# Two reorderings in a fused two-block kernel: first masks ahead of a token shift in the recurrent mixer, value transposes behind the first query group and late value products later in attention

## The chip, the cores and the metric
One Trainium2 chip, one core. The metric is the device time of one execution in microseconds (us); lower is better. Its engines run programs of their own, in order, and meet through semaphores: TensorE (PE in the profile; its weight loads are PEld), VectorE (DVE), ScalarE (ACT), GpSimd (POOL) and SyncE (SP), which only issues the weight transfers here.

## The reference, cut to what matters
Two transformer blocks in f32 over 256 tokens (272 with 16 meta tokens in the first block) of width 2048. Block one is a mixer, half short convolution and half a recurrence (RWKV-7: sixteen heads of 64), and a gated feed-forward with a convolution. Block two is a sliding-window attention with 32 query heads, 8 key heads and a sink per head, and a feed-forward of the same kind.

```python
def step(s, inp):                      # the recurrence, per head
    r_t, w_t, k_t, v_t, a_t, b_t = inp
    sa = jnp.einsum('bhvk,bhk->bhv', s, a_t)
    s = s * w_t[:, :, None, :] + sa[..., None] * b_t[:, :, None, :] + v_t[..., None] * k_t[:, :, None, :]
    return s, jnp.einsum('bhvk,bhk->bhv', s, r_t)
...
q, k, v = split_cols(h @ w_in, SWA_SPLITS)
s = einsum(q, kb) * HEAD_DIM ** -0.5 + bias          # masked to the window
p = softmax(concatenate([s, sink]))[..., :-1]
o = einsum(p, vb)
return o @ w_out
```

## The kernel before, in words
Every projection is `x @ W` with f32 weights that stream in as 512 KB chunks (two blocks of 128 rows by 512 columns). A ring of `RING = 4` chunks is filled by SP (`raw`). For each chunk ACT writes a rounded copy (`high`, line 525, tile `wh`) and DVE the rest (`low`, line 899, tile `wl`); TensorE multiplies in three passes, high by high, low by high, high by low. `high(n)` waits for the landing of chunk n and until TensorE has used chunk n-3 (`chunk_used`); `low(n)` waits for `high(n)` (`high_ready`); TensorE waits for `low(n)` (`low_ready`). Each engine's calls of `highs` and `lows` stand at fixed places among its other work, so a wait in one call holds back everything behind it on that engine.

**Mixer.** Projection groups 0 to 6 give the columns of the recurrence; group 6 holds the values v. `z_read(6)` (line 1007) takes them out of PSUM and `z_shift(6)` blends neighbouring tokens (a difference, line 1014, and four updates, line 1018, the last of which raises `z_ready`). The recurrence runs in five chunks of up to 64 tokens (c = 0 to 4). For each, TensorE makes the Gram products (line 1874) in banks 4 to 7, DVE masks them (`gak`, `grk`: `k_masked`; then `am`, `ga`, `grb`: `b_masked`; lines 1247 to 1253), TensorE turns four tiles by products with an identity (`heads`, line 1797: k into bank 6, am into 7, v into 4, b into 5), and a chain of levels l (products P, joins J) inverts the masked matrix. Between these steps TensorE is given pieces of the remaining projections, halves of chunks (`fill`, lines 1786 to 1788). `inverse_lengths(c, half)` (lines 1056 and 1058: a maximum and a reciprocal) serves a later chunk; `refill(s)` on DVE does a piece of the convolution and the `low` conversions that are due in that slot.

**Attention.** The projection `in2` has six groups of eight chunks: group 0 keys, group 1 values, groups 2 to 5 queries. The first two are interleaved over in2 chunks 0 to 15; group 2 has chunks 16 to 23. Its first half runs, then eight transposes of the values (line 1973) go to banks 4 and 5, ACT copies them out (`vt`, line 842), the second half follows, and TensorE waits for `vt_ready` before the loop. DVE's program here is: read group 0, `lows` of chunks 17 to 20, read group 1, `lows` of 21 to 26, and only then `evacuate_in2(2)` (line 1500), which raises `q_first` for the first scores. Neither version changes that DVE order. The loop has 18 turns over 16 pairs of heads. In turn i TensorE has `values(i-2)` (line 2037), `scores(i)` (line 2017), a piece of projection (`fill_attention`, lines 1997 to 2002), `turn(i-1)`, the transposes of the normalised weights (line 2028), and a second piece. Turns 0 to 12 have two halves of a chunk in each piece, turns 13 to 15 one in each, turn 16 two and none. ACT does per turn `out_high(i-2)` (line 868), the due `high`s, `softmax_pair(i)` (line 855) and `turn_out(i-1)` (line 863). DVE does `out_low(i-2)` (line 1544), its part of `scores(i)` (lines 1524 and 1526), the due `low`s and `normalise(i)`. `turn(i)` waits for `pn_ready` of pair i and for `o_low` of the pair before it, since both use bank 7.

Of the kernel before, what the change touches and what calls it, by code (L numbers as in the profile page):

```python
# [24 lines left out]
ACT = mybir.ActivationFunctionType  # L25

P = 128
# [116 lines left out]
def program(nc, d):  # L144
    with ExitStack() as ctx:
# [249 lines left out]
        def grams(b):  # L395

            return ps[:, b:b + 2, :].rearrange("p b (f x t) -> p (b f) x t", f=4, x=2)
# [116 lines left out]
        def _(act):  # L514
# [12 lines left out]
            def highs(first, count, slot=0):  # L527
                if isinstance(first, int):
                    count = clamp(first, count)
                for c in range(count):  # L530
                    high(first + c, (slot + c) % RING)
# [305 lines left out]

            bias_src = bass.AP(scratch.tensor, 0, [[1, P], [384, N_HEADS], [1, SEQ]])
            act.dma_start(bias[:], bias_src).then_inc(bias_landed, 16)
            highs(FIRST["in2"] + 19, 4, 3)  # L840
            act.wait_ge(v_turned, 1)
            act.activation(vt[:], ps[:, 4:6, :], ACT.Copy).then_inc(vt_ready, 1)
            highs(FIRST["in2"] + 23, 5, 3)

            def softmax_pair(i):

# [46 lines left out]
        def _(dve):  # L893
# [116 lines left out]
            def z_shift(g):  # L1010
                dve.wait_ge(group_read, g + 1)
                if g:
                    dve.wait_ge(z_ready, g)
                dve.tensor_tensor(zd[:], z[:, 4 * g:4 * g + 4, 0:L], z[:, 4 * g:4 * g + 4, 1:L + 1],
                                  ALU.subtract).then_inc(dve_step, 1)
                dve.wait_ge(dve_step, steps.add())
                for k in range(4 * g, 4 * g + 4):
                    last = dve.scalar_tensor_tensor(z[:, k, 1:L + 1], zd[:, k % 4], vcol("mu", k), z[:, k, 1:L + 1],
                                                    ALU.mult, ALU.add)
                last.then_inc(z_ready, 1)  # L1020
# [100 lines left out]
            factors(0)  # L1121
            lows(55, 5, 3)
            z_read(6)
            z_shift(6)
            dve.wait_ge(bias_stored, 16)

            def conv_read(s):
# [115 lines left out]
            for c in range(N_RC):  # L1243
                s = SLOT[c, "gram"]
                conv_read(s)
                dve.wait_ge(gram_done, 2 * c + 1)
                dve.tensor_tensor(gak[:], grams(6)[:, :, 0], over(gmask[:, 0], RT), ALU.mult)
                dve.tensor_tensor(grk[:], grams(6)[:, :, 1], over(gmask[:, 1], RT), ALU.mult).then_inc(k_masked, 1)
                dve.wait_ge(gram_done, 2 * c + 2)
                dve.tensor_tensor(am[0][:], grams(4)[:, :, 0], over(lmask[:, 0], RT), ALU.mult).then_inc(am_ready, 1)  # L1250
                dve.tensor_copy(ga[:], grams(4)[:, :, 0]).then_inc(dve_step, 1)
                ga_step = steps.add()
                dve.tensor_tensor(grb[:], grams(4)[:, :, 1], over(gmask[:, 1], RT), ALU.mult).then_inc(b_masked, 1)
                dve.wait_ge(am_ready, level(c, 0))
                dve.tensor_tensor(tt[:], am[0][:], over(identc[:], RT), ALU.add).then_inc(tt_ready, 1)
                dve.wait_ge(dve_step, ga_step)
                level_matrix(c, 1)
                refill(s)

                s = SLOT[c, "turn"]  # L1260
                conv_read(s)
                dve.wait_ge(am_turned, c + 1)
                dve.tensor_tensor(tn[:], bank(7), over(identc[:], RT), ALU.add).then_inc(tn_ready, 1)
                if c:
                    bonus_keys(c - 1)
                if c == LAST:
                    bonus_keys(c)
                refill(s)

                for l in range(1, LEVELS[c]):  # L1270
                    s = SLOT[c, f"P{l}"]
                    conv_read(s)
                    if l + 1 < LEVELS[c]:
                        level_matrix(c, l + 1)
                    if l == 3 and c < LAST:
                        factors(c + 1)
                    if c < 2 and l in (1, 4):
                        inverse_lengths(2 * c + 1 + l // 4, 0)
                    if c < 2 and l in (2, 5):
                        unit_keys(2 * c + 1 + l // 5)  # L1280
                    if c and l == 4:
                        inverse_spread(c - 1, 1)
                    if c and l == 5:
                        bonuses(c - 1, 7)
                    refill(s)

                    s = SLOT[c, f"J{l}"]
                    conv_read(s)
                    if l < LEVELS[c] - 1:
                        dve.wait_ge(dn_done, not_last(c, l))  # L1290
                        dve.wait_ge(tn_ready, turned_level(c, l - 1))
                        dve.tensor_tensor(tn[:], tn[:], bank(5), ALU.add).then_inc(tn_ready, 1)
                    dve.wait_ge(dt_done, inner(c, l))
                    dve.wait_ge(tt_ready, level(c, l - 1))
                    dve.tensor_tensor(tt[:], tt[:], bank(6), ALU.add).then_inc(tt_ready, 1)
                    if c < 2 and l in (1, 4):
                        inverse_lengths(2 * c + 1 + l // 4, 1)
                    if c and l == 3:
                        inverse_spread(c - 1, 0)
                    if 0 < c < LAST and l == 4:  # L1300
                        unit_y(c - 1)
                    refill(s)

                s = SLOT[c, "update"]
                conv_read(s)
                if c == LAST:
                    bonuses(c - 1, 7)
                    bonuses(c, 5)
                    inverse_spread(c - 1, 1)
                    unit_y(c - 1)  # L1310
                refill(s)

                s = SLOT[c, "output"]
                conv_read(s)
                if c < LAST:
                    dve.wait_ge(s_done, c + 1)
                    ends = pend[:, c].unsqueeze(2).broadcast_to([P, RT, C])
                    if c:
                        dve.wait_ge(st_ready, c)
                        dve.tensor_tensor(st[:], st[:], bank(5), ALU.add).then_inc(dve_step, 1)  # L1320
                        dve.wait_ge(dve_step, steps.add())
                    dve.tensor_tensor(st[:], st[:] if c else bank(5), ends, ALU.mult).then_inc(st_ready, 1)
                else:
                    gated_bonus(TG, TA, LAST - 1)
                    gated(TG, TA, LAST - 1)
                refill(s)
# [258 lines left out]
        def _(pe):  # L1585
# [272 lines left out]
            for c in range(N_RC):  # L1858
# [24 lines left out]
                pe.wait_ge(am_ready, level(c, 0))  # L1883
                heads(7, [(lambda f: am[0][:, f], lambda f: identc[:])], am_turned)
                pe.wait_ge(b_masked, c + 1)
                pe.wait_ge(z_ready, 7)
                heads(4, [(lambda f: z[:, 20 + f, 1 + t0:1 + t0 + n], lambda f: identc[:])], vb_turned, rows=n)
                if c < LAST:
                    heads(5, [(lambda f: bk[:, f, 0], lambda f: identc[:])], b_turned)
                finish(c, "turn")  # L1890

# [74 lines left out]
                chunks_of("in2", n0, n0 % RING, 0, x_of(SEQ), SEQ, range(c0, c1))  # L1966

            pe.wait_ge(group_read, G0["in2"] + 1)
            in2_piece(2, 0, 4)
            pe.wait_ge(group_read, G0["in2"] + 2)  # L1970
            for kb in range(2):
                for g2 in range(4):
                    last = pe.transpose(ps[:, 4 + kb, P * g2:P * (g2 + 1)], vf[:, g2, QB * kb:QB * (kb + 1)], ident[:])
            last.then_inc(v_turned, 1)
            in2_piece(2, 4, 8)
            pe.wait_ge(vt_ready, 1)

            def fill_attention(part):

# [40 lines left out]
            def turn(i):  # L2020
                pe.wait_ge(pn_ready, i + 1)
                if i:
                    pe.wait_ge(pt_ready, i)
                    pe.wait_ge(o_low, i)
                for e in range(2):
                    for t, col in enumerate((0, QB + 1, 2 * QB + 1)):
                        x = 3 * e + t
                        last = pe.transpose(ps[:, 6 + x // 4, QB * (x % 4):QB * (x % 4 + 1)], pr[:, i % 2, e, col:col + QB], ident[:])
                last.then_inc(p_turned, 1)
# [12 lines left out]
            for i in range(N_PAIRS + 2):  # L2042
                if i == N_PAIRS + 1:
                    fill_attention(WEAVE_FILL[i][0])
                if i >= 2:
                    values(i - 2)
                if i < N_PAIRS:
                    scores(i)
                if i <= N_PAIRS:
                    fill_attention(WEAVE_FILL[i][0])  # L2050
                if 1 <= i <= N_PAIRS:
                    turn(i - 1)
                fill_attention(WEAVE_FILL[i][1])
# [119 lines left out]
```

## Time and profile before

| what | value |
|---|---|
| median of 3 runs | 2430.51 us (2430.29 to 2430.63) |
| the profiled execution's own time | 2430.03 us |
| its span, first to last instruction | 2428.2 us |
| TensorE busy | 2385.4 us, 98% |
| DVE / ACT / POOL busy | 1522.2 / 1038.2 / 167.3 us |
| mean granted TensorE clock | 0.997 of full |
| bytes moved | 406.04 MB, mean 167 GB/s |

A time in the rows is counted from the start of the span. An engine's idle time matters here only where it ends in idle time of TensorE.

### The profile page before, as it was taken

The page shows a single profiled execution, that of the slowest core. Times are in us where ns is not written, and L with a number is a line of the kernel's source. Part 1 is how long each engine was busy: PE and PEld are TensorE (multiplying, and loading weights), DVE is VectorE, ACT ScalarE, POOL GpSimd, SP SyncE. Part 2 cuts the span into 40 slices and gives each one's busy share as a digit, 9 for nine tenths or more (in the row PEclk, how much of TensorE's full clock was granted, in tenths as well). Part 3 has the DMA queues.
Part 4 walks back from the last instruction along what each step waited for, and adds up shares of the span by engine and source line. Part 5 has one row for each costly group of instructions (what it writes and reads, how often), then busy time and mean ns, then how long its engine had stood idle before and what let it go on. Part 6 is the DMA issues. An engine that isn't in the chain of part 4 may idle for free.

```text
span 2428.2 us, 54209 instructions
## 1 busy us (share of the span) xinstructions
PE 2385.4 (98%) x21898; PEld 2294.9 (95%) x21898; DVE 1522.2 (63%) x1951; ACT 1038.2 (43%) x1292; POOL 167.3 (7%) x197
## 2 busy tenths in 40 slices
PE   7999999999999999999999999999999999999996
PEld 7999999999999999999889999899999999998896
DVE  6577665665866666565444666647767667664444
ACT  5543333344544443444444456555444344344442
POOL 2000000001400000000000310015000000000001
PEclk9999999999999999999999999999999999999998
DMA  7443222345455555555555473354555555555553
GB/s 240 153 163 123 82 89 91 112 142 183 148 191 181 184 182 180 186 183 183 189 186 189 148 252 131 117 179 154 191 185 179 190 184 179 191 186 188 190 185 104
DMA packets 116224, 406.04 MB, mean 167 GB/s; under 512 B 12624, under 2 KB 19760, under 8 KB 115824
## 3 DMA queue, kind: packets, MB, share of 16 engines
q1 hardware_dynamic: 109248, 392.22, 49.4%
q10 hardware_dynamic: 6832, 11.68, 1.4%
q8 instruction: 118, 1.93, 0.3%
q14 instruction: 26, 0.21, 0.0%
HBM read 401.69 MB, written 2.15 MB: 166 GB/s over the span
## 4 chain that ended last, share of the span: by engine, by line
PE 93%; DVE 4%; ACT 1%; issue 1%; ACTq 0%; DVEq 0%
PE ps L1637 17%; PE ps L1638 17%; PE ps L1639 17%; PE ps L1633 11%; PE ps L1635 6%; PE ps L1797 5%; PE ps L1786 2%; PE ps L1609 2%; PE ps L1610 2%; PE ps L1611 2%; PE ps L1788 2%; PE ps L1787 2%; DVE wl L899 1%; PE ps L2000 1%; DVE h L1382 1%; PE ps L2002 1%
## 5 line engine op out<-in xcount | busy, mean ns | idle before, releaser
L899 DVE TENSOR_TENSOR wl<-raw,wh 128x1024 fp32r<-128x1024 f32 x744 | 915.5, 1239 | 761.0 <-ACT wh L525 760.4
L525 ACT ACTIVATE wh<-raw 128x1024 fp32r<-128x1024 f32 x744 | 781.0, 1057 | 1036.0 <-PE ps L1639 558.6
L1637 PE MATMUL ps<-xh,wh 128*128 128x256 f32 (+2 forms) x3456 | 979.6, 283 | 18.9 <-DVE xl L924 18.2
L1638 PE MATMUL ps<-xl,wh 128*128 128x256 f32 (+2 forms) x3456 | 976.6, 283 | 0.0
L1639 PE MATMUL ps<-xh,wl 128*128 128x256 f32 (+2 forms) x3456 | 976.3, 282 | 0.0
L1637 PEld LDWEIGHTS ps<-xh,wh 128*128 128x128 f32 x3456 | 652.9, 189 | 22.5 <-DVE wl L899 16.2
L1638 PEld LDWEIGHTS ps<-xl,wh 128*128 128x128 f32 x3456 | 653.9, 189 | 0.2
L1639 PEld LDWEIGHTS ps<-xh,wl 128*128 128x128 f32 x3456 | 652.5, 189 | 0.0
L1633 PE MATMUL ps<-act,wh 128*128 128x512 f32 x1056 | 369.7, 393 | 0.0
L1635 PE MATMUL ps<-act,wl 128*128 128x256 f32 x1056 | 294.6, 279 | 0.0
L1633 PEld LDWEIGHTS ps<-act,wh 128*128 128x128 f32 x1056 | 197.8, 187 | 47.3
L1635 PEld LDWEIGHTS ps<-act,wl 128*128 128x128 f32 x1056 | 197.9, 187 | 0.0
L1786 PE MATMUL ps<-xh,wh 128*128 128x260 f32 x384 | 114.6, 298 | 1.1 <-DVE cg L1142 0.9
L1787 PE MATMUL ps<-xl,wh 128*128 128x260 f32 x384 | 108.3, 282 | 0.0
L1788 PE MATMUL ps<-xh,wl 128*128 128x260 f32 x384 | 108.2, 282 | 0.0
L445 POOL TENSOR_TENSOR sq_sum<-sq_sum,sq 128x256 f32<-128x256 f32 (+2 forms) x104 | 84.1, 808 | 344.6 <-ACT sq L540 335.5
L1609 PE MATMUL ps<-act,wh 128*128 128x256 f32 x352 | 99.6, 283 | 0.0
L1610 PE MATMUL ps<-act,wh 128*128 128x256 f32 x352 | 99.4, 282 | 0.0
L1611 PE MATMUL ps<-act,wl 128*128 128x256 f32 x352 | 98.7, 280 | 0.0
L463 POOL COPY sq_sum<-sq 128x256 f32<-128x256 f32 (+2 forms) x8 | 4.1, 512 | 1237.4 <-ACT sq L540 1114.7
L1786 PEld LDWEIGHTS ps<-xh,wh 128*128 128x128 f32 x384 | 72.1, 188 | 6.0 <-DVE cg L1142 1.0
L1407 DVE SCALAR_TENSOR_TENSOR cv<-gt,vec,cv 128x256 f32<-128x256 f32 x176 | 73.3, 478 | 0.0
(270 smaller groups left out, 2749.9 us busy)
## 6 DMA issues: line engine op xcount, KB each, us to landing
raw<-in_gate_up SPq DMA_DIRECT2D x176, 512.0 KB, 3.8
raw<-in_down SPq DMA_DIRECT2D x176, 512.0 KB, 4.2
raw<-in_up SPq DMA_DIRECT2D x176, 512.0 KB, 3.8
raw<-in_w_in SPq DMA_DIRECT2D x104, 512.0 KB, 3.7
raw<-in_in SPq DMA_DIRECT2D x48, 512.0 KB, 3.7
raw<-in_w_out SPq DMA_DIRECT2D x32, 512.0 KB, 3.8
raw<-in_out SPq DMA_DIRECT2D x32, 512.0 KB, 3.7
bias<-bias_rows ACTq DMA_DIRECT2D x1, 4096.0 KB, 26.3
```

Source lines behind the costliest of these rows:

```text
L525: act.activation(wh[:, slot], raw[:, slot], ACT.Copy).then_inc(high_ready, 1)
L899: dve.tensor_tensor(wl[:, slot], raw[:, slot], wh[:, slot].bitcast(F32), ALU.subtract).then_inc(low_ready, 1)
L1609: pe.matmul(out, w_high, hi, start=(k == 0), stop=False)
L1610: pe.matmul(out, w_high, lo, start=False, stop=False)
L1633: pe.matmul(ps[:, 4 * parity + m, :], w_high, hi.rearrange("p s n -> p (s n)"), start=(k == 0), stop=False)
L1635: last = pe.matmul(out, w_low, hi[:, 0], start=False, stop=(k == 2 * per - 1))
L1637: pe.matmul(out, w_high, hi, start=(k == 0), stop=False)
L1638: pe.matmul(out, w_high, lo, start=False, stop=False)
L1639: last = pe.matmul(out, w_low, hi, start=False, stop=(k == 2 * per - 1))
L1786: pe.matmul(out, w_high, hi, start=(k == 0), stop=False)
L1787: pe.matmul(out, w_high, lo, start=False, stop=False)
L1788: last = pe.matmul(out, w_low, hi, start=False, stop=(x < 96 and k == KT - 1))
```

## The change
In the mixer, for chunk 0 alone, `z_shift(6)` leaves its place right behind `z_read(6)` and goes behind the mask that raises `b_masked`; TensorE turns b (bank 5) ahead of v (bank 4) in that chunk. In chunks 0 and 1, the second half of `inverse_lengths` goes behind the `refill` of the same slot. In attention all eight chunks of query group 2 run before the value transposes, which now go to banks 6 and 7; ACT makes two more `high`s ahead of the copy of `vt` (19 to 24 instead of 19 to 22) and leaves 25 to 27 behind it; the wait for `vt_ready` moves from ahead of the loop to the first `turn`. In turns 13 to 15 `values(i-2)` goes behind `scores(i)`, and in turn 16 behind the projection piece, straight ahead of `turn(15)`.

```diff
-            highs(FIRST["in2"] + 19, 4, 3)
+            highs(FIRST["in2"] + 19, 6, 3)
             act.wait_ge(v_turned, 1)
-            act.activation(vt[:], ps[:, 4:6, :], ACT.Copy).then_inc(vt_ready, 1)
-            highs(FIRST["in2"] + 23, 5, 3)
+            act.activation(vt[:], ps[:, 6:8, :], ACT.Copy).then_inc(vt_ready, 1)
+            highs(FIRST["in2"] + 25, 3, 1)
...
             z_read(6)
-            z_shift(6)
...
                 dve.wait_ge(gram_done, 2 * c + 1)
+                if c == 0:
+                    dve.wait_ge(group_read, 7)
                 dve.tensor_tensor(gak[:], grams(6)[:, :, 0], over(gmask[:, 0], RT), ALU.mult)
...
                 dve.tensor_tensor(grb[:], grams(4)[:, :, 1], over(gmask[:, 1], RT), ALU.mult).then_inc(b_masked, 1)
+                if c == 0:
+                    z_shift(6)
...
-                    if c < 2 and l in (1, 4):
-                        inverse_lengths(2 * c + 1 + l // 4, 1)
                     if c and l == 3:
                         inverse_spread(c - 1, 0)
                     if 0 < c < LAST and l == 4:
                         unit_y(c - 1)
                     refill(s)
+                    if c < 2 and l in (1, 4):
+                        inverse_lengths(2 * c + 1 + l // 4, 1)
...
                 pe.wait_ge(b_masked, c + 1)
-                pe.wait_ge(z_ready, 7)
+                if c == 0:
+                    heads(5, [(lambda f: bk[:, f, 0], lambda f: identc[:])], b_turned)
+                    pe.wait_ge(z_ready, 7)
                 heads(4, [(lambda f: z[:, 20 + f, 1 + t0:1 + t0 + n], lambda f: identc[:])], vb_turned, rows=n)
-                if c < LAST:
+                if 0 < c < LAST:
                     heads(5, [(lambda f: bk[:, f, 0], lambda f: identc[:])], b_turned)
...
             pe.wait_ge(group_read, G0["in2"] + 1)
-            in2_piece(2, 0, 4)
+            in2_piece(2, 0, 8)
             pe.wait_ge(group_read, G0["in2"] + 2)
             for kb in range(2):
                 for g2 in range(4):
-                    last = pe.transpose(ps[:, 4 + kb, P * g2:P * (g2 + 1)], vf[:, g2, QB * kb:QB * (kb + 1)], ident[:])
+                    last = pe.transpose(ps[:, 6 + kb, P * g2:P * (g2 + 1)], vf[:, g2, QB * kb:QB * (kb + 1)], ident[:])
             last.then_inc(v_turned, 1)
-            in2_piece(2, 4, 8)
-            pe.wait_ge(vt_ready, 1)
...
                     pe.wait_ge(pt_ready, i)
                     pe.wait_ge(o_low, i)
+                else:
+                    pe.wait_ge(vt_ready, 1)
...
                 if i == N_PAIRS + 1:
                     fill_attention(WEAVE_FILL[i][0])
-                if i >= 2:
+                if 2 <= i < 13:
                     values(i - 2)
                 if i < N_PAIRS:
                     scores(i)
+                if 13 <= i < N_PAIRS:
+                    values(i - 2)
                 if i <= N_PAIRS:
                     fill_attention(WEAVE_FILL[i][0])
+                if i >= N_PAIRS:
+                    values(i - 2)
                 if 1 <= i <= N_PAIRS:
                     turn(i - 1)
```

## Rows read from the trace of the kernel before

**Rows 1.** The page: the chain of work that ended last, by engine.
```profile
PE 93%; DVE 4%; ACT 1%; issue 1%; ACTq 0%; DVEq 0%
```

**Rows 2.** Busy time by engine in attention turns 2 to 12 (columns: PE, PEld, DVE, ACT, POOL, clock, DMA).
```profile
1460.00:1550.00 90.00, 90.00 (x802) 82.41 (x802) 62.91 (x182) 54.46 (x133) 2.11 (x11) 1.00 0.40 129
```

**Rows 3.** Timeline, TensorE, mixer chunk 0 (start, duration, operation, count, idle before and releaser).
```profile
207.42 1.15 PE L1797 MATMUL ps<-identc,bk 64*64 64x64 f32 x32 [1.17 <-DVE grk L1248]
...
211.29 0.39 PE L1786 MATMUL ps<-xh,wh 128*128 128x260 f32 x1
```

**Rows 4.** Timeline, DVE, the same stretch.
```profile
203.09 1.29 DVE L1014 TENSOR_TENSOR zd<-z 128x1088 f32<-128x1088 f32 x1
...
206.68 0.68 DVE L1248 TENSOR_TENSOR grk<-ps,gmask 128x512 f32<-128x512 f32 x1
...
209.07 0.68 DVE L1255 TENSOR_TENSOR tt<-am,identc 128x512 f32<-128x512 f32 x1
```

**Rows 5.** Timeline, DVE, mixer chunk 0: the convolution's read behind level 4.
```profile
247.11 1.23 DVE L1142 TENSOR_TENSOR cg<-ps,rstd 128x1040 f32<-128x1040 f32 x1
```

**Rows 6.** Timeline, TensorE, value transposes and first scores of attention.
```profile
1433.83 1.04 PE L1973 MATMUL ps<-ident,vf 128*128 128x128 f32 x8
1434.63 0.36 PE L1637 MATMUL ps<-xh,wh 128*128 128x256 f32 x1
...
1445.97 0.27 PE L1639 MATMUL ps<-xh,wl 128*128 128x256 f32 x1
1446.85 0.93 PE L2017 MATMUL ps<-kf,qf 64*128 64x128 f32 x8 [0.61 <-DVE qf L1500]
```

**Rows 7.** Timeline, ACT: the copy of the turned values and the conversion behind it.
```profile
1434.91 1.03 ACT L842 ACTIVATE vt<-ps 128x1024 f32<-128x1024 f32 x1 [2.58 <-PE ps L1973]
1435.83 1.05 ACT L525 ACTIVATE wh<-raw 128x1024 fp32r<-128x1024 f32 x1
```

**Rows 8.** Timeline, DVE: conversion of in2 chunk 26, then the first query read.
```profile
1444.61 1.23 DVE L899 TENSOR_TENSOR wl<-raw,wh 128x1024 fp32r<-128x1024 f32 x1 [1.63 <-ACT wh L525]
1446.28 0.42 DVE L1500 SCALAR_TENSOR_TENSOR qf<-ps,rstd 128x256 f32<-128x256 f32 x1 [0.45 <-PE ps L1639]
```

**Rows 9.** Timeline, TensorE, attention turns 14 to 16.
```profile
1556.94 0.88 PE L2037 MATMUL ps<-pt,vt 128*64 128x128 f32 x12 [0.47 <-ACT pt L863]
1557.74 0.93 PE L2017 MATMUL ps<-kf,qf 64*128 64x128 f32 x8
...
1560.11 0.81 PE L2028 MATMUL ps<-ident,pr 128*128 128x128 f32 x6
1560.68 0.48 PE L1997 MATMUL ps<-yy,wh 128*128 128x512 f32 x1
...
1568.68 0.88 PE L2037 MATMUL ps<-pt,vt 128*64 128x128 f32 x12 [0.47 <-ACT pt L863]
...
1572.40 0.82 PE L2028 MATMUL ps<-ident,pr 128*128 128x128 f32 x6
```

**Rows 10.** Timeline, DVE, `out_low` in turn 14.
```profile
1558.28 0.42 DVE L1544 TENSOR_TENSOR yy<-ps,yy 128x256 fp32r<-128x256 f32 x1 [0.83 <-ACT yy L868]
```

**Rows 11.** Granted clock after the last matmul; matmul starts at both levels of it.
```profile
2409.00:2412.80 3.80, 0.00 (x1) 0.00 (x0) 3.18 (x4) 0.47 (x1) 1.42 (x2) 1.00 0.00 0
2413.00:2414.00 1.00, 0.00 (x0) 0.00 (x0) 1.00 (x2) 0.00 (x0) 1.00 (x2) 0.50 0.00 0
...
15.38 0.57 PE L1637 MATMUL ps<-xh,wh 128*128 128x272 f32 x1 [15.38 <-DVE xl L924]
...
19.60 0.43 PE L1637 MATMUL ps<-xh,wh 128*128 128x272 f32 x1
19.83 0.43 PE L1638 MATMUL ps<-xl,wh 128*128 128x272 f32 x1
...
20.23 0.29 PE L1637 MATMUL ps<-xh,wh 128*128 128x272 f32 x1
20.35 0.29 PE L1638 MATMUL ps<-xl,wh 128*128 128x272 f32 x1
```

## The prediction, written before the changed kernel had been run

> **What bounds the kernel now.** I read the page first. Its chain of work that ended last runs 93% of the span on TensorE [rows 1]: the time changes only where TensorE idles more or less. The stretch view of attention turns 2 to 12 shows what that is like: TensorE busy 90.00 of 90.00 us, at full clock [rows 2], so nothing moved inside it can gain. Then I looked in TensorE's timeline for idle gaps at the places of the change. There are five. One of 1.17 us stands ahead of the first turned tiles of mixer chunk 0, ended by the mask `grk` [rows 3]. One of 0.61 us stands ahead of the first scores, ended by the first query read [rows 6]. Three of 0.47 us stand ahead of `values` in turns 14, 15 and 16, ended by ACT's `turn_out` (two of the three are shown, and the middle one is like them) [rows 9]. Together that is 3.2 us, 0.13% of the time, and a little more in starts, because a gap counts from the modelled end of a matmul that the next would have overlapped. Measurement tells apart about 0.2%, 4.9 us. So the gains are small whatever happens, and the question is what the moves cost.
>
> **Part 1, masks ahead of the shift (mixer, chunk 0).** On DVE the shift's five instructions run from 203.09, and `grk` ends at 206.68 + 0.68 = 207.36; TensorE starts 0.06 later [rows 3, 4]. The change permutes ten DVE instructions without adding one: five of the shift, five of the masks. From `zd` at 203.09 to `tt` at 209.07 the total stays the same [rows 4], so `grk` ends near 204.4, `grb` near 206.2, the shift's last update near 209.15, and all behind it on DVE keeps its time. TensorE's gap goes: k, am and b are turned from 206.2 to 209.0 (three of four sets, which take (211.29 - 207.42) / 4 = 0.97 us each [rows 3]), then v waits for the shift until about 209.2, a new wait of 0.2 us, and the next piece starts at 209.2 + 1.03 = 210.25 instead of 211.29. Gain 1.0 us. What else could be late: ACT's copies of k, v and b (`kt`, `vb`, `bt`), but a 3 us projection piece lies between them and their users. Without that cover the gain would shrink by ACT's two copies, some 1.2 us. Bounds: 0.6 to 1.1.
>
> **Part 2, reciprocals behind `refill`.** At level 1 no conversion is due in that slot (chunk 0), or none and no convolution step (chunk 1): the order of instructions is unchanged. At level 4 of chunk 0 the order tt, reciprocal, `wl`, `cg` becomes tt, `wl`, reciprocal, `cg`; TensorE waits there for `cg`, which starts at 247.11 [rows 5], and the same work stands ahead of it. In chunk 1 only a 16-column reciprocal moves. Zero, from -0.3 to +0.3.
>
> **Part 3, transposes behind query group 2.** The eight transposes take 1434.63 - 1433.83 = 0.80 us [rows 6]. Moved behind the group, they could cover the wait for the first query read: the scores start at 1446.85 where they could have started at 1445.97 + 0.12 [rows 6], a gain of 0.76 us. But look at what is queued behind ACT's copy. Before, the copy was done at 1435.94 and the conversions 23 to 27 went on [rows 7], so DVE finished its conversion 26 at 1444.61 + 1.23 = 1445.84 and then waited only for TensorE before it read the queries at 1446.28 [rows 8]. After, `high` 25, 26 and 27 stand behind the copy, the copy waits for the transposes, and the transposes stand behind the whole group. DVE still has `low` 25 and `low` 26 ahead of the first query read, and the scores wait for that read. So a chain starts that TensorE cannot cover, as its next instruction is the scores:
>
> - transposes start at 1445.97 + 0.12 - 0.80 = 1445.27 (the group now runs on through the place they left)
> - copy: 1434.91 - 1433.83 = 1.08 later [rows 6, 7], 1446.35
> - `high` 25: 0.92 behind the copy's start [rows 7], 1447.27, ready at 1448.32
> - `low` 25: 1448.36; `low` 26 about 1.13 behind it (its 1.23 busy less the 0.1 by which such neighbours overlap [rows 7, 8]), 1449.5; `high` 26 (from 1448.2 to 1449.25) is in time
> - query read: 1450.6; the scores follow a query read's start by 1446.85 - 1446.28 = 0.57 [rows 6, 8], 1451.15
>
> Against 1446.85 that is 4.3 us late. TensorE idles from the transposes' end, 1445.27 + 1.04 = 1446.3, to 1451.15: 4.85 us, with two ready chunks (24 and, late, 25) lying behind the scores in its order. From there everything in the loop keeps its distances, since turns 2 to 12 hold no slack on TensorE to win it back [rows 2]. SP's queue: the transfers of chunks 29 and 30 wait for `low` 25 and 26 and go out some 6 us later, for conversions due later still; bound 0 to 0.5 us. Bounds of the part: +3.9 (if conversions pack closer) to +5.0. I take 4.3.
>
> **The clock.** After the last matmul of the kernel, at 2409.00, the granted clock stayed at full until past 2412.8 and was half at 2413, some 3.9 us on [rows 11]. The new gap is 4.85 us, longer than that by 1 us. At the kernel's start matmuls ran at half clock (1.2 GHz) from 15.38 to about 20.1, 4.75 us, 0.23 apart, then 0.12 apart [rows 11]. So, if the clock falls, work goes at about 0.53 of its rate for a stretch; 4.75 us of it cost 4.75 x 0.47 = 2.2 us. Bounds 0 and 2.2; as the gap exceeds the 3.9 us by only 1 us, I take a short fall, 1.0 us. The Trainium skill (TensorE: Matmul & The Clock Gate, What's actually happening) says that the throttled clock is the default and only activity releases it; by that the clock may fall or hold here depending on where the gap lies, which no row before decides, and the sum would be 1.0 us less or 1.2 us more than mine.
>
> **Part 4, `values` later (turns 13 to 16).** The three waits come from a closed loop: `values(i-2)`, `out_high`, `out_low`, DVE's scores of pair i, softmax, `turn_out(i-1)`, `values(i-1)`. Its period is (1568.68 - 1556.94) / 2 = 5.87 us [rows 9], while TensorE's own work in a turn is 1560.68 - 1556.94 = 3.74 plus one more piece. A piece of one half is 1560.11 - 1557.74 less the scores' 0.86 (their 0.93 busy less the overlap of 0.07 that values show too), 1.5, and the turn's work 5.24. Every edge of the loop is a data dependence or the order on ACT and DVE, and none is changed. What changes is the start: `values(11)` goes behind scores, 1557.74 - 1556.94 = 0.80 for values and 0.86 for scores, so the loop starts 0.86 later. In turns 14 and 15 TensorE waits as before, now between scores and values. In turn 16, `values(14)` no longer waits, since the two-half piece goes ahead; but `turn(15)` stands right behind it and needs `out_low(14)`, whose end is 1558.28 + 0.42 - 1556.94 = 1.76 us behind the start of `values` [rows 9, 10], of which TensorE covers 0.80 by values themselves. The sum, from the start of turn 13 to `turn(15)`: before, 3 x 5.87 + (1572.40 - 1568.68) = 21.33 [rows 9]; after, 0.86 + 2 x 5.87 + 0.80 + 1.5 + 0.57 + 1.5 + 2.9 + 1.8 = 21.7 (waits of the loop, `values(13)`, a piece, `turn(14)`, a piece, the two halves of turn 16 as 3.72 - 0.80, and `values(14)` to the end of `out_low(14)`). A loss of 0.35, bounds -1.9 (all three waits gone, 3 x 0.63) to +1.0.
>
> **Rivals.** *The clock holds through the gap* (2434.2): for it, that the fall after the last matmul took 3.9 us and the gap has 4.85; against it, the same two numbers. *The clock stays down as long as at the start*: +2.2, 2436.4. *Part 4 works*: the waits vanish, 0.35 becomes -1.9, 2433.0; against it is the closed loop, whose length the rows give. *The other side, faster*: the conversions 25 and 26 do not gate the scores. That would need the copy to begin 4.3 us before I put it, at 1442.0, while the group still runs; from there on the transposes cover the query read and part 3 gives -0.8. With part 1 and 4 as summed it is 2429.1, and with part 4 at its best 2426.8, not even then 0.2% faster. Nothing in the rows speaks for it: only a copy that need not wait for the group's end would do it. *The change does nothing visible* would take the same.
>
> **How the numbers follow.** Against the profiled execution (2430.03, of which the span is 2428.2 and 1.8 lies around it) the sum is -1.0 + 0 + 4.3 + 0.35 + 1.0 = +4.7; the median of the runs is 0.5 above that execution, so 2430.5 + 4.7 = 2435.2. Chances: short fall of the clock 0.40 (2434.6 to 2436.2); clock holds 0.31 (2433.8 to 2434.7); long fall 0.17 (2435.8 to 2437.2); part 4 works 0.06; conversions do not gate 0.04; the rest 0.02. The bound to slower is 2435.4: the long fall lies above it, nearly half of the short one, and a little of the holding case: 0.38. Faster needs under 2425.6: 0.02. Range 2433.4 to 2437.0, which leaves out the last cases and the upper end of the long fall.
>
> **What would show it.** Right: TensorE's first turned tile at 206.2 with a short wait ahead of the turned v; a gap of about 4.8 us ahead of the first scores, released by DVE's query read, with two conversions right ahead of that read on DVE and the copy ahead of them on ACT; two waits for `pt` of about 0.5 us in turns 14 and 15 and one of 0.9 to 1 us ahead of `turn(15)`, released by DVE's `yy`; the granted clock under 1 somewhere near 1450. Wrong: first scores near 1446, or a clock that stays at half for tens of microseconds.

## The result, and the profile after

The changed kernel takes 2435.97 us (median of 11 runs, 2435.12 to 2437.0) against 2430.49 us of the kernel before (11 runs): ratio 1.0021, 95% interval 1.0012 to 1.0030. It is slower by about 0.2%; 2435.2 was forecast, with a range of 2433.4 to 2437.0. Its profiled execution took 2435.20 us, of which the span is 2433.4. In the experiments below, two single executions took 3206.37 us (part 4 alone) and 5030.39 us (part 2 alone) and are left out of their ratios, though not of their medians.

In the changed kernel's lines `values` is line 2042, scores 2020, the value transposes 1978, `turn` 2033, the query read 1503, `out_low` 1547, DVE's scores 1527 and 1529; `heads` is 1800, the mixer's pieces 1789 to 1791. The timeline of TensorE in mixer chunk 0 answers to [rows 3]:

```profile
206.19 1.15 PE L1800 MATMUL ps<-identc,bk 64*64 64x64 f32 x32
207.18 1.10 PE L1800 MATMUL ps<-identc,am 64*64 64x64 f32 x32
208.11 1.10 PE L1800 MATMUL ps<-identc,bk 64*64 64x64 f32 x32
209.34 1.15 PE L1800 MATMUL ps<-identc,z 64*64 64x64 f32 x32
...
210.41 0.39 PE L1789 MATMUL ps<-xh,wh 128*128 128x260 f32 x1
```

The gap of 1.17 us ahead of the first turned tile is gone, b is turned ahead of v, and v waits a little (1.23 us from b to v, where neighbours stand 0.93 to 0.99 apart). The next piece of projection (called the mixer piece below) starts 0.88 us earlier.

TensorE at the value transposes answers to [rows 6]:

```profile
1444.43 1.04 PE L1978 MATMUL ps<-ident,vf 128*128 128x128 f32 x8
1450.25 1.18 PE L2020 MATMUL ps<-kf,qf 64*128 64x128 f32 x8 [4.79 <-DVE qf L1503]
...
1458.48 0.93 PE L2020 MATMUL ps<-kf,qf 64*128 64x128 f32 x8
```

A new idle gap of 4.79 us stands ahead of the first scores, released by DVE's query read. ACT (first fence) and DVE (second) in the same stretch, in place of [rows 7, 8], show why:

```profile
1445.50 1.02 ACT L842 ACTIVATE vt<-ps 128x1024 f32<-128x1024 f32 x1 [8.27 <-PE ps L1978]
1446.42 2.94 ACT L525 ACTIVATE wh<-raw 128x1024 fp32r<-128x1024 f32 x3
```

```profile
1447.51 2.36 DVE L899 TENSOR_TENSOR wl<-raw,wh 128x1024 fp32r<-128x1024 f32 x2 [9.02 <-ACT wh L525]
1449.78 0.41 DVE L1503 SCALAR_TENSOR_TENSOR qf<-ps,rstd 128x256 f32<-128x256 f32 x1
```

ACT waited 8.27 us for the transposes with three conversions behind that wait; DVE waited 9.02 us for the first of them with the query read behind. Both were idle while TensorE ran most of the query group, and then TensorE was idle while they did two conversions that could have been done by then. (`high(n)` needs its ring slot free: the wait is for chunk n-4, one earlier than the section on the kernel before says. So conversion 26 needs chunk 22 and may run while TensorE is at chunk 23, the last of the group; the run with both conversions ahead of the copy, below, shows this: VectorE is at its part of conversion 26 at 1443.06, and the group runs until 1444.54.)

The view of stretches (columns as in [rows 2]: length of the stretch, busy time of PE, PEld, DVE, ACT, POOL, then the granted clock) shows the gap, what follows it, and recovery:

```profile
1445.50:1450.20 4.70, 0.00 (x0) 0.00 (x0) 2.69 (x4) 4.68 (x5) 0.00 (x0) 1.00 0.13 18
1450.90:1454.10 3.20, 3.20 (x17) 2.74 (x14) 2.64 (x10) 1.00 (x5) 0.00 (x0) 0.50 0.73 253
1454.30:1458.00 3.70, 3.70 (x33) 3.70 (x33) 2.27 (x6) 1.73 (x5) 0.19 (x1) 1.00 0.48 142
```

The clock was full through the gap and half (1.2 GHz) behind it: 17 matmuls in 3.20 us, against 33 in 3.70 us right after. From the first to the second scores it is 8.23 us (1450.25 to 1458.48). Before, with the first at 1446.85 [rows 6], it was 6.72:

```profile
1453.57 0.93 PE L2017 MATMUL ps<-kf,qf 64*128 64x128 f32 x8
```

The tail, TensorE in turns 14 to 16, answers to [rows 9]:

```profile
1555.97 0.93 PE L2020 MATMUL ps<-kf,qf 64*128 64x128 f32 x8
1556.83 0.88 PE L2042 MATMUL ps<-pt,vt 128*64 128x128 f32 x12
...
1567.06 0.93 PE L2020 MATMUL ps<-kf,qf 64*128 64x128 f32 x8
1568.35 0.88 PE L2042 MATMUL ps<-pt,vt 128*64 128x128 f32 x12 [0.36 <-ACT pt L863]
...
1575.62 0.88 PE L2042 MATMUL ps<-pt,vt 128*64 128x128 f32 x12
1577.53 0.84 PE L2033 MATMUL ps<-ident,pr 128*128 128x128 f32 x6 [1.03 <-DVE yy L1547]
```

Of three waits for `pt` two are left (one is shown, the other is like it), now between scores and `values`, and a wait of 1.03 us stands ahead of `turn(15)`. Turn 13 began like this before:

```profile
1551.07 0.88 PE L2037 MATMUL ps<-pt,vt 128*64 128x128 f32 x12
```

Added up from the two profiles, as shifts against before: the mixer piece -0.88 (211.29 to 210.41), first scores +3.40 (1446.85 to 1450.25), start of turn 13 +4.90 (1551.07 to 1555.97), `turn(15)` +5.13 (1572.40 to 1577.53), end of span +5.2. The steps between them are the parts: -0.9 mixer, +4.3 the chain ahead of the scores, +1.5 half clock, +0.2 tail. The clock's part differs from one execution to the next, as the section on the scatter shows.

### The profile page after: what moved, and what is told of

Same layout as the page of the kernel before. It is cut to its first block, busy times and chain, and to the rows that moved or that the text cites. A ratio compares the mean times of both kernels' runs of the same rounds, so it can differ in the third digit from the quotient of the medians.

```text
span 2433.4 us, 54204 instructions
## 1 busy us (share of the span) xinstructions
PE 2387.6 (98%) x21898; PEld 2296.5 (94%) x21898; DVE 1521.5 (63%) x1951; ACT 1037.9 (43%) x1292; POOL 167.2 (7%) x197
## 4 chain that ended last, share of the span: by engine, by line
PE 93%; DVE 4%; ACT 1%; issue 1%; POOL 0%; ACTq 0%; POOLq 0%; DVEq 0%
PE ps L1640 17%; PE ps L1641 17%; PE ps L1642 17%; PE ps L1636 11%; PE ps L1638 6%; PE ps L1800 5%; PE ps L1789 2%; PE ps L1612 2%; PE ps L1613 2%; PE ps L1614 2%; PE ps L1790 2%; PE ps L1791 2%; DVE wl L899 1%; PE ps L2003 1%; DVE h L1385 1%
```

## The experiments

The ratios below are to the kernel before, run on the same chip in turn with it. Part 1, part 3, part 4 and the filled gap were run on one chip, the others on a second. On both the kernel before was less steady than above: medians 2431.11 and 2430.63 us, from 2429.7 up to 2434.6. So differences under 1 us are read from the traces, as distances between two points of TensorE's timeline. Such distances repeat to some hundredths where the granted clock is the same in both.

### Part 3 alone

The kernel before with only the lines of the diff from `highs(FIRST["in2"] + 19` to the `vt_ready` wait in `turn`:

```diff
-            in2_piece(2, 0, 4)
+            in2_piece(2, 0, 8)
...
-            in2_piece(2, 4, 8)
-            pe.wait_ge(vt_ready, 1)
```

> The kernel before with part 3 alone: transposes behind query group 2, copy of the turned values behind conversion 24. My theory (two conversions stand behind that copy on ScalarE and ahead of the query read on VectorE): first scores about 5.8 us behind the start of the transposes, a TensorE gap of 4.8 us released by the query read, the start of turn 13 later by 4.2 us less nothing, plus what half clock costs (1.5 us in the changed kernel's profile): 2430.5 + 4.2 + 1.5 to 2.2 = 2436.2 to 2436.9, so more than the whole change. Rival (the loss comes from the moves in the mixer and the late values, or from the sum of all): this part alone gives 2429.7 to 2431.

Measured: 2438.13 us (6 runs, 2435.73 to 2440.88), ratio 1.0031 (1.0018 to 1.0043); the profiled execution took 2436.77. TensorE:

```profile
1446.25 1.03 PE L1973 MATMUL ps<-ident,vf 128*128 128x128 f32 x8
1452.07 1.65 PE L2015 MATMUL ps<-kf,qf 64*128 64x128 f32 x8 [4.79 <-DVE qf L1500]
```

The same 5.82 us from transposes to scores and the same gap, so the rival that the loss comes from the other parts (2429.7 to 2431) is out. Counted from the mixer piece, which starts at 212.32 in this profile, the first scores come 4.19 us later than before (1452.07 - 212.32 against 1446.85 - 211.29), and the second follow after 8.26 us, 1.54 more than before. Together that is 5.7 us, about what the whole change loses in these two steps (4.3 + 1.5). The median is above the expected 2436.2 to 2436.9: three of the six runs lie from 2439.49 to 2440.88, none of them was profiled, and what they hold stays open. By the times alone, part 3 can't be told from the whole change: their intervals overlap.

### Part 1 alone

The kernel before with `z_shift(6)` behind `grb` in chunk 0 and the turned b ahead of v:

```diff
             z_read(6)
-            z_shift(6)
...
+                if c == 0:
+                    z_shift(6)
```

> The kernel before with part 1 alone: chunk 0's masks ahead of the last shift. My theory: the projection piece behind the turned tiles starts 0.9 us earlier and nothing downstream takes it back: 2429.6. Rival (the shift, now behind the masks, makes a later step wait and gives the 0.9 us back): 2430.5.

Measured: 2429.62 us, ratio 0.9995 (0.9986 to 1.0005). The time alone does not settle 0.9 us. The trace does. From the start of `z_read(6)` on DVE to the mixer piece on TensorE it is 8.60 us (202.54 to 211.14), where it was 9.52 before (201.77 to 211.29), a gain of 0.92. And of the kernel before's idle times of TensorE, the one for `grk` is absent and every other is as before (`cg` 0.9, `qf` 0.6, three times `pt`, 1.4 in all), so nothing downstream took the gain back.

### Part 4 alone

```diff
-                if i >= 2:
+                if 2 <= i < 13:
                     values(i - 2)
                 if i < N_PAIRS:
                     scores(i)
+                if 13 <= i < N_PAIRS:
+                    values(i - 2)
...
+                if i >= N_PAIRS:
+                    values(i - 2)
```

> The kernel before with part 4 alone: values behind scores in turns 13 to 15 and behind the piece in turn 16. My theory (a closed loop through ScalarE and VectorE sets the pace; the order on TensorE does not shorten it): from the start of turn 13 to the last turn's transposes 21.5 to 21.7 us against 21.33 before, time 2430.7. Rival (the scores cover the wait): three waits of 0.63 us vanish, 2428.6.

Measured: 2432.39 us, ratio 1.0007 (0.9997 to 1.0016). From the start of turn 13 at 1552.57 to `turn(15)` at 1574.16 it is 21.59 us, 21.33 before: a loss of 0.26 us. TensorE at the end of it:

```profile
1572.26 0.88 PE L2037 MATMUL ps<-pt,vt 128*64 128x128 f32 x12
1574.16 0.85 PE L2028 MATMUL ps<-ident,pr 128*128 128x128 f32 x6 [1.03 <-DVE yy L1544]
```

The medians lie further apart than that, 1.3 us on that chip, and the median is 1.7 us above the expected 2430.7. The profiled execution (2431.84 us) holds a stretch at half clock of its own in the mixer, told of in the last section, so the time is no measure of this part; the distance is. Whether such stretches make up the whole of the difference no run shows.

### The gap filled with dummy matmuls

The changed kernel, with matmuls whose result nobody reads in the gap:

```diff
             last.then_inc(v_turned, 1)
+            for _ in range(19):
+                pe.matmul(ps[:, 4, 0:P], ones[:], ones[:], start=True, stop=True)
```

> The changed kernel with 19 dummy matmuls (a result that nobody reads, in a bank that the scores overwrite) behind the value transposes, some 4.4 us of work inside the 4.8 us gap. If half clock behind the gap costs 1.5 us or more, as the profile of the changed kernel has it: first scores at the same distance from the transposes (5.8 us), granted clock at full throughout, time 2434.0 and the scatter between runs gone. If the clock costs nothing and the scatter has another source: 2435.97, as the changed kernel.

Measured: 2433.95 us, ratio 1.0013 (1.0004 to 1.0022); ten of the eleven runs lie from 2433.25 to 2434.67, and one, not profiled, at 2438.47. TensorE, and the stretch behind the scores:

```profile
1445.27 4.41 PE L1981 MATMUL ps<-ones 128*128 128x128 f32 x38
1450.22 0.93 PE L2022 MATMUL ps<-kf,qf 64*128 64x128 f32 x8 [0.54 <-DVE qf L1503]
```

```profile
1450.90:1458.00 7.10, 7.07 (x61) 6.39 (x58) 5.04 (x17) 3.64 (x10) 0.19 (x1) 1.00 0.51 183
```

The scores start where they did, the clock stays full, and from first to second scores it is 6.80 us (1450.22 to 1457.02), where the changed kernel took 8.23. So the half clock, and not the gap, accounts for the 1.4 us between these two profiles, and work that computes nothing takes it back. By the medians it is 2.0 us (2435.97 and 2433.95), but these are two series of runs whose intervals against the kernel before overlap, so 2.0 is a rough figure. The Trainium skill (TensorE: Matmul & The Clock Gate, What's actually happening) says that the throttled clock is the default and that activity releases it. This trace agrees: with TensorE busy through 4.41 us of the gap, the granted clock is 1.00 behind it. The last section has a fall in a busy stretch, which that rule does not lead one to expect.

### One conversion more ahead of the copy

```diff
-            highs(FIRST["in2"] + 19, 6, 3)
+            highs(FIRST["in2"] + 19, 7, 3)
...
-            highs(FIRST["in2"] + 25, 3, 1)
+            highs(FIRST["in2"] + 26, 2, 2)
```

> The changed kernel with ScalarE's conversion 25 ahead of the copy of the turned values as well (26 and 27 behind it). By my theory the chain is one conversion shorter on each engine: first scores 4.7 us behind the start of the transposes instead of 5.82, a gap of 3.7 us instead of 4.79. Time 2434.9 if the clock still falls each time, 2432.9 if it never does; which of the two a 3.7 us gap does, no run has shown. Rival (it is the transposes' new place or bank, not the conversions): scores stay 5.8 us behind, 2436.

Measured: 2435.81 us, ratio 1.0019 (1.0009 to 1.0028), where 2434.9 was expected if the clock falls. The runs lie in two heaps (five from 2434.08 to 2434.62, six from 2435.81 to 2437.77), and the profiled one, 2434.26, is in the lower. TensorE:

```profile
1444.54 1.04 PE L1978 MATMUL ps<-ident,vf 128*128 128x128 f32 x8
1449.23 0.93 PE L2020 MATMUL ps<-kf,qf 64*128 64x128 f32 x8 [3.65 <-DVE qf L1503]
```

4.69 us, as expected: the chain is 1.13 us shorter by one conversion. But the clock still falls, later:

```profile
1445.70:1449.20 3.50, 0.00 (x0) 0.00 (x0) 1.59 (x3) 3.48 (x4) 0.00 (x0) 1.00 0.04 15
1449.30:1450.90 1.60, 1.57 (x14) 1.20 (x15) 1.29 (x4) 0.53 (x1) 0.00 (x0) 1.00 0.51 125
1451.00:1454.30 3.30, 3.30 (x18) 3.30 (x17) 2.46 (x10) 1.87 (x8) 0.19 (x1) 0.50 0.37 109
```

### Both conversions ahead of the copy

```diff
-            highs(FIRST["in2"] + 19, 6, 3)
+            highs(FIRST["in2"] + 19, 8, 3)
...
-            highs(FIRST["in2"] + 25, 3, 1)
+            highs(FIRST["in2"] + 27, 1, 3)
```

> The changed kernel with conversions 25 and 26 ahead of the copy, 27 behind it. By my theory VectorE reads the queries as soon as the group ends, the transposes cover that read, the gap is under 0.1 us (scores 0.8 to 0.9 us behind the transposes' start) and the clock never falls: 2430.5 - 0.9 - 0.76 + 0.23 = 2429.1. Rival (the copy itself, or its bank, delays ScalarE's first softmax and so the loop): scores early, but the start of turn 13 gains less than 1.6 us on the kernel before.

Measured: 2429.39 us, ratio 0.9993 (0.9984 to 1.0002), an interval that takes in the kernel before. TensorE, and DVE's last conversion and query read:

```profile
1444.54 1.03 PE L1978 MATMUL ps<-ident,vf 128*128 128x128 f32 x8
1445.50 0.93 PE L2020 MATMUL ps<-kf,qf 64*128 64x128 f32 x8
```

```profile
1443.06 1.23 DVE L899 TENSOR_TENSOR wl<-raw,wh 128x1024 fp32r<-128x1024 f32 x1 [1.63 <-ACT wh L525]
1444.74 0.42 DVE L1503 SCALAR_TENSOR_TENSOR qf<-ps,rstd 128x256 f32<-128x256 f32 x1 [0.45 <-PE ps L1642]
```

The scores follow the transposes by 0.96 us, without an idle gap, and DVE waits for TensorE again, not TensorE for DVE. Counted from the mixer piece behind the turned tiles, the first scores come 0.55 us earlier than before (1445.50 - 210.49 against 1446.85 - 211.29), not the 0.76 worked out, as the transposes cost 0.96 us there and not 0.80. By the same count the start of turn 13 gains only 0.30 us (1549.97 - 210.49 against 1551.07 - 211.29). What takes the other 0.25 stands behind the query read on DVE:

```profile
1450.13 0.35 DVE L1527 CUSTOM_DVE_ANT_0 sc<-ps,bias,nsinks 128x128 f32<-128x128 f32 x1 [4.10 <-DMA bias<-bias_rows]
```

```profile
1459.87 0.88 PE L2042 MATMUL ps<-pt,vt 128*64 128x128 f32 x12 [0.19 <-ACT pt L863]
```

DVE's first scores (first fence) wait 4.10 us for the transfer of the bias rows, issued at 1419.7 and landed 30.4 us later (26.3 in the profile of before, where it was in time). Softmax and `values` of turn 2 come late behind it, and TensorE waits 0.19 us for them at 1459.87 (second fence). That the transfer is the cause of this wait is read from the order of the work, and no run tests it alone. So the rival (turn 13 gains less than 1.6 us; it gains 1.10, 1551.07 to 1549.97) holds as to its sign: a new wait takes a part of the gain. Nothing in the trace speaks for its cause, ACT's copy and bank. With the query read early, the bias transfer is what is late next, and neither I nor the forecast's faster rival had it. Still, between the medians of the two series of runs a change of two counts takes back 6.6 us.

### The loop cut

On top of that, DVE's scores ahead of `out_low` in turns 13 to 15, and in turn 16 `values` between the two halves of the piece:

```diff
-                if i >= 2:
+                if i >= 2 and not 13 <= i < N_PAIRS:
                     out_low(i - 2)
...
                     scores(i)
+                    if i >= 13:
+                        out_low(i - 2)
...
+                if i == N_PAIRS:
+                    fill_attention(WEAVE_FILL[i][0][:1])
+                    values(i - 2)
+                    fill_attention(WEAVE_FILL[i][0][1:])
```

> As the run with both conversions ahead, and in turns 13 to 15 VectorE does its scores ahead of out_low, with TensorE's scores still ahead of values; in turn 16 values stand between the two halves of the piece. If the loop values, out_high, out_low, VectorE scores, softmax, turn_out is what sets 5.76 to 5.87 us a turn, taking out_low out of it leaves TensorE's own 5.24 us a turn, and from the start of turn 13 to the last transposes it is 19.4 to 19.7 us against 21.33 before: 2429.1 - 0.23 - 1.7 = 2427.2. Rival (ScalarE is the bound: softmax, turn_out, a conversion and out_high, 4.4 us of work a turn with its waits): 21 us or more, 2429.

Measured: 2427.23 us (2426.45 to 2430.1), ratio 0.9985 (0.9976 to 0.9994), the fastest of all and, with an interval that ends below 1, clear of the kernel before. TensorE in turns 13 to 16:

```profile
1551.08 0.93 PE L2022 MATMUL ps<-kf,qf 64*128 64x128 f32 x8
1551.93 0.88 PE L2044 MATMUL ps<-pt,vt 128*64 128x128 f32 x12
...
1556.40 0.93 PE L2022 MATMUL ps<-kf,qf 64*128 64x128 f32 x8
1557.26 0.88 PE L2044 MATMUL ps<-pt,vt 128*64 128x128 f32 x12
...
1568.45 0.88 PE L2044 MATMUL ps<-pt,vt 128*64 128x128 f32 x12
1570.77 0.82 PE L2035 MATMUL ps<-ident,pr 128*128 128x128 f32 x6
```

A turn takes 5.32 us (1551.08 to 1556.40; TensorE's own work in a turn was summed to 5.24) and none of them waits; from turn 13 to `turn(15)` it is 19.69 us against 21.33 before and 21.56 in the changed kernel. So the loop through `out_low` set the pace of turns 13 to 15, and ACT did not. Of the 1.87 us between 21.56 and 19.69, about 0.9 is in turns 14 and 15 (two periods of 5.76 against 5.32), and the rest in turn 16, whose order changed too. (In this profile the bias transfer made DVE wait 1.78 us ahead of its first scores, which cost TensorE nothing.)

### Part 2 alone

```diff
-                    if c < 2 and l in (1, 4):
-                        inverse_lengths(2 * c + 1 + l // 4, 1)
...
                     refill(s)
+                    if c < 2 and l in (1, 4):
+                        inverse_lengths(2 * c + 1 + l // 4, 1)
```

> The kernel before with part 2 alone: the second half of the reciprocals behind the slot's conversions. My theory: only the order of a reciprocal and a conversion changes in one place, the same work stands ahead of the convolution's read, TensorE's wait of 0.86 us ahead of its first piece of the next group stays: 2430.5. Rival (the conversion was late there): that wait shrinks, up to 0.9 us off.

Measured: 2431.35 us, ratio 1.0001 (0.9992 to 1.0010). DVE in place of [rows 5], then TensorE's wait there:

```profile
243.93 1.22 DVE L899 TENSOR_TENSOR wl<-raw,wh 128x1024 fp32r<-128x1024 f32 x1
...
245.39 1.75 DVE L1058 RECIPROCAL rkr<-rkr 128x256 f32<-128x256 f32 x1
247.06 1.18 DVE L1142 TENSOR_TENSOR cg<-ps,rstd 128x1040 f32<-128x1040 f32 x1
```

```profile
248.29 0.39 PE L1786 MATMUL ps<-xh,wh 128*128 128x260 f32 x1 [0.87 <-DVE cg L1142]
```

The order changed, the wait did not (0.86 before). The median is 0.85 us above the expected 2430.5, with four runs above 2432.5 that were not profiled; the profiled execution took 2429.93.

### Where the scatter of the runs lies

The runs of the changed kernel spread over 1.9 us. Two more profiled executions of it, and one of the kernel with one conversion more ahead:

> The changed kernel unaltered, another profiled execution. If the scatter of its runs (2435.1 to 2437.0) comes from where the stretch of half clock falls against the work: the distance from transposes to first scores stays 5.82 us, the distance from the first to the second scores (8.23 us in the first profile, 6.72 before) differs by what the half clock covers, and it accounts for the difference in time to within 0.3 us. If the scatter lies elsewhere, that distance stays 8.23.

> As the run beside it, a third profiled execution of the changed kernel: the same test of where the scatter lies.

> The kernel with one more conversion ahead of the copy, another profiled execution. Its 11 runs lay in two heaps, 2434.1 to 2434.6 and 2435.8 to 2437.8. If the heaps are one and two stretches of half clock, a slow one shows a stretch twice as long behind the gap or a second one elsewhere; if they are something else, the clock record is that of the first profile (one stretch from 1450.95 to 1454.36).

The two of the changed kernel took 2436.18 and 2436.03 us, the first profiled one 2435.20. TensorE and the clock in the slower:

```profile
1449.91 1.65 PE L2020 MATMUL ps<-kf,qf 64*128 64x128 f32 x8 [4.79 <-DVE qf L1503]
...
1459.44 0.93 PE L2020 MATMUL ps<-kf,qf 64*128 64x128 f32 x8
```

```profile
1445.20:1449.20 4.00, 0.00 (x0) 0.00 (x0) 2.04 (x2) 3.98 (x5) 0.00 (x0) 1.00 0.00 0
1449.50:1456.00 6.50, 6.09 (x29) 5.44 (x30) 4.63 (x16) 2.68 (x9) 0.19 (x1) 0.50 0.60 177
1456.30:1459.00 2.70, 2.70 (x26) 2.70 (x25) 1.19 (x2) 1.06 (x1) 0.00 (x0) 1.00 0.34 138
```

Here half clock lasted 6.8 us (1449.3 to 1456.1) instead of some 3.4 (1450.8 to 1454.2), and the distance between first and second scores is 9.53 us; in the other it is 8.77 (1450.51 to 1459.28), again with 6.8 us of half clock (1448.2 to 1455.0), of which 2.3 lie in the gap and cost nothing. From transposes to scores all three have 5.82. In the slower one the distance grew by 1.30 us, the transposes came 0.34 us earlier (1444.09 against 1444.43), and 1.30 - 0.34 = 0.96 is the difference in time, 0.98. In the other, 0.54 + 0.26 = 0.80 against 0.83. The third kernel took 2435.49 us against 2434.26 in its first profile, with a distance of 9.16 us (1449.61 to 1458.77) against 8.32 (1449.23 to 1457.55): 0.84, and transposes 0.38 later, 1.22 against 1.23. Its half clock was again one long stretch behind the gap, 6.8 us where the first profile of that kernel has 3.4, and there is no second one elsewhere. So in these three pairs the clock accounts for most of the difference in time (1.30 us where 0.34 had been won ahead of the transposes and the times differ by 0.98; 0.54 of 0.83; 0.84 of 1.23), and the time follows how much work the stretch covers. Taken alone, the distance misses the 0.3 us of the expectation by little in one pair (1.30 against 0.98) and keeps it in the other (0.54 against 0.83). The rest, 0.26 to 0.38 us, arose ahead of the transposes. That the heaps are the two lengths of the stretch is likely but not shown: 2435.49 lies between them, and no run of the upper heap was profiled.

## Why the prediction was right, point by point

The prediction counts five idle gaps of TensorE at the places of the change. There was a sixth, the 0.86 us ahead of the piece that waits for `cg`, which it names under part 2 alone; that gap is in the changed kernel as well.

- **Part 1**, -1.0: it measured -0.9. DVE's `gak` started 0.14 us behind the end of `z_read` where 0.04 was put, and the rest came within 0.2 us of what was worked out, the new wait ahead of v included.
- **Part 2**, zero: shown by the run of that part alone.
- **Part 3**, +4.3: shown. From transposes to scores 5.88 was summed (1445.27 to 1451.15) and 5.82 measured, in each of five profiles of that order. The cause was tested from both sides: one conversion out of the chain took off 1.13 us, two took off all of it, and the part alone carries the loss. The transposes' new place and bank cost no more than some 0.2 us: in the run with both conversions ahead they keep both.
- **The clock**, +1.0 of 0 to 2.2: that the clock would fall was right, and the term was mis-sized. It measured 1.5, 2.8 and 2.05 us in three profiles of the changed kernel (first to second scores, less 6.72), and 1.5 with part 3 alone. Two readings of mine failed. I took the 3.9 us behind the last matmul as the time that a fall needs, and expected it inside the gap, about 1 us before its end. In the three profiles the clock fell 5.3, 4.2 and 2.5 us behind the modelled end of the transposes: 0.5 us after the scores had started, 0.6 us before and 2.3 us before. So the reason given for a short fall, a gap 1 us longer than 3.9, decided nothing. And the upper bound, 4.75 us at half clock from the start of the kernel, was too low: half clock lasted 6.8 us in two of the three, and cost 2.8 us in one, where 2.2 was the bound. That the clock was half at the start I had read from the spacing of the matmuls alone (0.23 us, then 0.12); the profile's clock column gives 1.00 there. The case that the clock holds, given 0.31, did not occur: the fastest of 11 runs is 1.2 us above the 2433.95 of the filled gap. With some 2 us for this term the sum would have been about 1 us higher, and this is the main part of what stands between 2435.2 and 2435.97. That the term was still near enough for the range to hold is in part luck, since it rested on these readings.
- **Part 4**, +0.35: it measured +0.23 in the whole change and +0.26 alone. The closed loop was right, and the run that takes `out_low` out of it shows it. Its period is 5.76 us in the changed order, not 5.87 (1562.59 to 1568.35), as DVE's scores no longer wait for TensorE's and start while `out_low` ends, 0.34 us behind its start where it was 0.44.

The rival of the faster side named what would be needed, a copy that does not hold back conversions 25 and 26, and gave 2429.1 for it; the run that did it took 2429.39, with some 0.2 us each, behind the bias transfer and in the transposes, as what it had not counted. The forecast gave 0.38 to a loss of over 0.2%, 0.02 to a gain of that size and so 0.60 to neither. The measured ratio, 1.0021, is just beyond that line, with an interval that takes in both sides, so one result says little about these chances.

## What to carry to other kernels

Before an instruction that waits is moved on an engine, list what stands behind it there, and what stands behind each of those on the next engine: here one copy held two conversions, these held a read of PSUM, and that held TensorE, for an intended gain of 0.8 us. Where engines wait for one another in a ring, moving work on the engine that idles only shifted the wait here (+0.2 us), and taking an edge out of the ring shortened it (-1.6 us). And the idle gaps of TensorE of 3.65 and 4.8 us cost 1.5 to 2.8 us more in clock: where such a gap can't be avoided, it can be filled.

## What the runs showed of the hardware

- The clock's fall is tied neither to the gap's end nor to one delay behind the last work: in three profiles of the changed kernel it came 2.5 to 5.3 us behind the transposes. In the profile with a gap of 3.65 us TensorE had been back at work for about 1.7 us at full clock before the clock fell, and it then stayed at half for some 3.4 us of unbroken work (18 matmuls in 3.30 us, where the full clock had 33 in 3.70).
- It also fell without any gap, in the mixer, in two of the profiles (part 4 alone, and the loop cut), at the same place. Busy time and clock there, of the loop cut:

```profile
508.00:513.00 5.00, 5.00 (x109) 4.87 (x110) 4.97 (x11) 1.13 (x2) 0.00 (x0) 1.00 0.31 108
513.70:516.80 3.10, 3.10 (x26) 2.87 (x26) 2.70 (x3) 1.41 (x2) 0.00 (x0) 0.50 0.04 5
517.00:520.00 3.00, 3.00 (x61) 2.83 (x60) 2.39 (x9) 1.18 (x3) 0.00 (x0) 1.00 0.44 164
```

  TensorE shows 5.00 of 5.00 us busy ahead of it, in part with small matmuls (64x64 and 64x16) of the mixer. It costs some 1.4 us: the transposes stand at 1445.90 in that profile and at 1444.54 in the one without it (both conversions ahead, the same up to there; the mixer piece stands at 210.48 and 210.49). Such a stretch may account for runs of the kernel before near 2432; none of those was profiled, and why the clock falls there in some executions and not in others stays open.
